# The first expert block's rows made by products of the resident x with marked lanes, and w2 of expert 0 waiting for its place alone

## The reference

```
h = modulate(rms_norm(x, norm_ffn_g[l]), sh_f, sc_f).reshape(-1, d)          # 512 x 1024
...
g_logits = (h @ w_group).astype(jnp.float32) + b_group.astype(jnp.float32)   # 4 groups
g_idx = jnp.argmax(g_logits, axis=-1)
e_logits = ((h @ w_router).astype(jnp.float32) + b_router...)                # 4 x 8 experts
within = jnp.take_along_axis(e_logits, g_idx[:, None, None], axis=1)[:, 0]
top_vals, top_idx = lax.top_k(within, MOE_TOP_K)                             # 2 of 8
...
for e in range(MOE_EXPERTS):                                                 # 32 experts
    hid = jax.nn.silu(h @ w1[e]) * (h @ w3[e])                               # 1024 -> 512
    out = out + gates[:, e:e + 1] * (hid @ w2[e]).astype(jnp.float32)        # 512 -> 1024
x = x + g_f * f.reshape(x.shape)
return rms_norm(x, final_norm_g)
```

## Time and profile before

| | before |
|---|---|
| median of 3 runs | 1003.13 us (1002.63 to 1018.23) |
| profiled execution | 1004.4 us |
| its span | 1002.5 us |
| mean granted TensorE clock | 0.949 of 2.4 GHz |
| TensorE busy | 871.5 us (87%) |
| VectorE / ScalarE / GpSimd busy | 423.2 / 245.4 / 138.1 us |
| moved by DMA | 263.58 MB |

### The profile page before, as it was taken

How to read it: one execution, slowest core, us unless ns; L and a number is a source line. 1 busy time by engine, 2 the same in 40 slices (tenths; PEclk the granted TensorE clock), 3 DMA queues, 4 the chain that set the end, 5 groups by cost and what they waited for, 6 DMA issues and landing times.

```text
span 1002.5 us, 12704 instructions
## 1 busy us (share of the span) xinstructions
PE 871.5 (87%) x4421; PEld 435.2 (43%) x4421; DVE 423.2 (42%) x1082; ACT 245.4 (24%) x560; POOL 138.1 (14%) x373
## 2 busy tenths in 40 slices
PE   4699999999989989999879999999999977666860
PEld 2355546644445555446633444444444433332320
DVE  3586888544388646035721323222221321211226
ACT  5411023103267664114010111111111211111102
POOL 1401002020000000001010222122121321221210
PEclk9799999999999999999789999999999988989995
DMA  9952204366700320034859999999999999999946
GB/s 341 348 169 49 84 0 120 101 199 245 269 2 1 105 106 1 20 148 168 336 212 390 377 418 418 419 421 420 420 421 421 418 418 418 418 418 419 419 189 251
DMA packets 52613, 263.58 MB, mean 263 GB/s; under 512 B 11171, under 2 KB 13531, under 8 KB 25696
## 3 DMA queue, kind: packets, MB, share of 16 engines
q1 hardware_dynamic: 40320, 246.04, 60.9%
q0 software_dynamic: 12080, 17.00, 6.1%
q10 hardware_dynamic: 176, 0.05, 0.0%
HBM read 265.66 MB, written 22.01 MB: 287 GB/s over the span
## 4 chain that ended last, share of the span: by engine, by line
PE 43%; issue 38%; POOL 6%; DVE 5%; DMA 4%; ACT 2%; POOLq 1%; SPq 0%; DVEq 0%; ACTq 0%
PE PS L729 14%; PE PS L992 6%; PE PS L918 4%; DMA BIG<-in_w_mod 3%; POOL held L578 2%; PE PS L925 2%; PE PS L639 2%; PE PS L694 2%; PE PS L955 2%; POOL BIG L587 2%; PE PS L1078 1%; PE PS L964 1%; DMA BIG<-xh_d,gidx 1%; DVE sml L1941 1%; PE PS L802 1%
## 5 line engine op out<-in xcount | busy, mean ns | idle before, releaser
L729 PE MATMUL PS<-BIG 128*128 128x512 f32 (+2 forms) x352 | 139.8, 553 | 0.0
L729 PEld LDWEIGHTS PS<-BIG 128*128 128x128 f32 x352 | 64.2, 190 | 68.6 <-issue 68.3
L1178 PE MATMUL PS<-BIG,GM 128*64 128x512 f32 x336 | 79.0, 613 | 7.2 <-DMA BIG<-in_moe_w 6.0
L1159 PE MATMUL PS<-S5Z,QKV 128*128 128x512 f32 x192 | 83.4, 592 | 0.0
L1156 PE MATMUL PS<-BIG,QKV 128*64 128x512 f32 x288 | 64.2, 596 | 7.2 <-DMA BIG<-in_moe_w 5.5
L578 POOL TENSOR_TENSOR held<-held 1x1 f32<-1x1 f32 x147 | 27.1, 185 | 310.3 <-PE PS L1132 169.7
L2300 DVE TENSOR_TENSOR QKV<-PS,QKV 64x512 f32<-64x512 f32 x50 | 34.4, 688 | 81.3 <-PE PS L1178 51.9
L1481 ACT ACTIVATE QKV<-PS,fcp 128x128 f32<-128x128 f32 x128 | 48.3, 458 | 63.1 <-PE PS L1132 63.1
L1149 PE MATMUL PS<-BIG,QKV 128*32 128x256 f32 x768 | 47.8, 400 | 12.8 <-DMA BIG<-in_moe_w 12.8
L2280 DVE TENSOR_SCALAR QKV<-PS,fcp 128x128 f32<-128x128 f32 x128 | 43.7, 405 | 33.2 <-PE PS L1132 33.2
L992 PE MATMUL PS<-BIG 128*128 128x512 f32 x128 | 56.1, 595 | 0.0
(11 more groups left out here) (480 smaller groups left out, 1158.2 us busy)
## 6 DMA issues: line engine op xcount, KB each, us to landing
BIG<-in_moe_w SPq DMA_DIRECT2D x84, 1024.0 KB, 21.2
BIG<-in_moe_w SPq DMA_DIRECT2D x21, 2048.0 KB, 22.9
S5Z<-in_moe_w SPq DMA_DIRECT2D x40, 1024.0 KB, 18.7
BIG<-in_w_mod SPq DMA_DIRECT2D x12, 2048.0 KB, 7.9
S5Z<-in_moe_w SPq DMA_DIRECT2D x10, 2048.0 KB, 22.8
BIG<-in_w_in SPq DMA_DIRECT2D x3, 2048.0 KB, 17.4
QKV<-in_x SPq DMA_DIRECT2D x8, 512.0 KB, 11.3
BIG<-in_w_out SPq DMA_DIRECT2D x2, 2048.0 KB, 11.8
```

What stands on the lines that cost most here:

```text
L729: ins = mm(dst[:, c0:width], hT[:, k, tok], wslot(n, width)[:, k, c0:width], start=(k == 0), stop=(k == KD - 1))
L1159: ins = mm(bank(2 + m), hgT[:, k, :], w13(side)[:, m, k, :], start=(k == 0), stop=(k == KD - 1))
L1178: ins = mm(PS[64 * n:64 * n + 64, 2560:3072], hidT[:, k % 2, 64 * (k // 2):64 * (k // 2) + 64], w2s(side)[:, k, 512 * n:512 * (n + 1)], st ...
```

## The change

In place of the gather from DRAM, the turning and the copies by both engines, the rows of block 0 are made so: VectorE writes, for each of the four token tiles, a matrix `own` (128 tokens x 64 lanes) that has the token's reciprocal `sml[:, 36 + t]` where the token's larger position equals block 0's first position plus the lane, and zero elsewhere. TensorE multiplies the resident `XN` with it, 8 slices of the model dimension (read with a step of 8 elements) times 4 token tiles, 32 products; the result is turned already. ScalarE copies it in two parts (signals `picked` and `hg_tr`) to `hgT0`, which lies in the upper half of `GM`, with the same scale and shift, and gives both `hgT_a` and `hgT_d`. Block 0's up-projection reads `hgT0` and stands ahead of the wait for `routed` on TensorE. GpSimd's first gather is that of block 1. On VectorE the weights of the two choices are computed ahead of the wait for `filled`. On SyncE w2 of expert 0 no longer waits for `hg_in`.

```
--- before.py
+++ after.py
@@ -213,6 +213,9 @@
         ysb = QKV[:, 6144:7168]
         hid = GM[:, 0:512]
         hidT = GM[:, 512:1024].rearrange("p (k s) -> p k s", k=4)
+        own = GM[:, 0:256].rearrange("p (t l) -> p t l", t=NLT)
+        lanes_at = GM[:, 256:320]
+        hgT0 = GM[:, 512:1024].rearrange("p (k s) -> p k s", k=KD)
         sg = wglu[:, :, :].rearrange("p k n -> p (k n)")
         rt = S5Z[:, 8192:11520]
         logit = rt[:, 0:144].rearrange("p (t e) -> p t e", t=NLT)
@@ -415,7 +418,6 @@
                 load13(0, 2, 0, piece)
             sp.wait_ge(sem("slots"), 2)
             sp.wait_ge(sem("routed"), 1)
-            sp.wait_ge(sem("hg_in"), 16)
             load2(0, 2)
             last = sp.value_load(btab[0:1, NBLK + 2:NBLK + 3], min_val=0, max_val=NTRI) + 3
 
@@ -560,7 +562,7 @@
             pool.wait_ge(sem("xh_out"), 16 * NLT)
             st.settle()
             pool.wait_ge(sem("slots"), 1)
-            pool.tensor_copy(gidx[:, :], slots[:, 0:1, 0]).then_inc(sem("gidx"), 1)
+            pool.tensor_copy(gidx[:, :], slots[:, 1:2, 0]).then_inc(sem("gidx"), 1)
             pool.wait_ge(sem("gidx"), 1)
             pool.indirect_dma_start(hg, None, xh_d, bass.IndirectOffsetOnAxis(gidx[:, 0:1], 0),
                                     bounds_check=LAT - 1, oob_is_err=False).then_inc(sem("hg_in"), 16)
@@ -583,7 +585,7 @@
             def gather(b):
 
                 pool.tensor_copy(gidx[:, :], entry(b, 0)).then_inc(sem("gidx"), 1)
-                hold(sem("gidx"), b + 1)
+                hold(sem("gidx"), b)
                 pool.indirect_dma_start(hg, None, xh_d, bass.IndirectOffsetOnAxis(gidx[:, 0:1], 0),
                                         bounds_check=LAT - 1, oob_is_err=False).then_inc(sem("hg_in"), 16)
 
@@ -597,8 +599,6 @@
                 pool.indirect_dma_start(pair_d, bass.IndirectOffsetOnAxis(sidx[:, 0:1], 0), ysb, None,
                                         bounds_check=TOPK * LAT, oob_is_err=False).then_inc(sem("y_sc"), 16)
 
-            hold(sem("hg_tr"), 1)
-            gather(1)
             hold(sem("hg_tr"), 2)
             gather(2)
 
@@ -1104,7 +1104,15 @@
             mm(bank(6, NE, 192), qb_b[0:NE, :], opp128[0:NE, :], start=True, stop=False)
             mm(bank(6, NE, 192), hb_b[0:NE, :], tri128[0:NE, :], start=False, stop=True)
             mm(bank(6, NE, 224), hb_b[0:NE, :], ident[0:NE, 0:NE], start=True, stop=True).then_inc(sem("place"), 1)
-            warm(8)
+            warm(5)
+            pe.wait_ge(sem("own"), 1)
+            for k in range(KD):
+                for t in range(NLT):
+                    ins = mm(bank(k // 4, 64, (k % 4) * P), XN[:, t, :].rearrange("p (q k) -> p k q", k=KD)[:, k, :], own[:, t, :],
+                             start=(t == 0), stop=(t == NLT - 1))
+                if k == KH - 1:
+                    ins.then_inc(sem("picked"), 1)
+            ins.then_inc(sem("hg_tr"), 1)
             for k in range(TOPK):
                 pe.wait_ge(sem("spread"), k + 1)
                 for t in range(NLT):
@@ -1115,19 +1123,11 @@
             mm(PS[0:1, 3584:3584 + NBLK], ones[0:NE, 0:1], cmph[0:NE, :], start=True, stop=False)
             mm(PS[0:1, 3584:3584 + NBLK], wexp[0:NE, :], cmpq[0:NE, :], start=False, stop=False)
             mm(PS[0:1, 3584:3584 + NBLK], wexp[0:NE, :], cmpf[0:NE, :], start=False, stop=True).then_inc(sem("bt"), 1)
-            warm(3)
-
-            pe.wait_ge(sem("routed"), 1)
-
-            mixed = pe.value_load(btab[0:1, NBLK:NBLK + 1], min_val=0, max_val=NTRI) + 1
-            small = pe.value_load(btab[0:1, NBLK + 1:NBLK + 2], min_val=0, max_val=NTRI) + 2
-            last = pe.value_load(btab[0:1, NBLK + 2:NBLK + 3], min_val=0, max_val=NTRI) + 3
 
             def turn_rows(b):
-                pe.wait_ge(sem("hg_in"), 16 * b + 16)
-                if not isinstance(b, int) or b >= 1:
-                    pe.wait_ge(sem("hgT_a"), b)
-                    pe.wait_ge(sem("hgT_d"), b)
+                pe.wait_ge(sem("hg_in"), 16 * b)
+                pe.wait_ge(sem("hgT_a"), b)
+                pe.wait_ge(sem("hgT_d"), b)
                 for k in range(KD):
                     ins = tr(bank(k // 4, P, (k % 4) * P), hg.rearrange("p (q k) -> p k q", k=KD)[:, k, :], ident)
                 ins.then_inc(sem("hg_tr"), 1)
@@ -1152,12 +1152,20 @@
                         for m in range(2):
                             if size == "half":
 
+                                few = hgT0[:, k, :] if isinstance(b, int) else hgT[:, k, 64:128]
                                 r = slice(64 * m, 64 * m + 64)
-                                ins = mm(PS[r, 1024:1536].rearrange("p (m h) -> p m h", m=2), hgT[:, k, 64:128],
+                                ins = mm(PS[r, 1024:1536].rearrange("p (m h) -> p m h", m=2), few,
                                          w13(side)[:, :, k, 256 * m:256 * m + 256], start=(k == 0), stop=(k == KD - 1))
                             else:
                                 ins = mm(bank(2 + m), hgT[:, k, :], w13(side)[:, m, k, :], start=(k == 0), stop=(k == KD - 1))
                     ins.then_inc(sem("w13_used"), 1)
+
+            up(0, "half", 0, 1)
+            pe.wait_ge(sem("routed"), 1)
+
+            mixed = pe.value_load(btab[0:1, NBLK:NBLK + 1], min_val=0, max_val=NTRI) + 1
+            small = pe.value_load(btab[0:1, NBLK + 1:NBLK + 2], min_val=0, max_val=NTRI) + 2
+            last = pe.value_load(btab[0:1, NBLK + 2:NBLK + 3], min_val=0, max_val=NTRI) + 3
 
             def turn_hid(b, size):
                 pe.wait_ge(sem("hid"), b + 1)
@@ -1192,10 +1200,6 @@
                 down(b - 1, size_before, j, i)
                 turn_hid(b, size)
 
-            warm(3)
-            turn_rows(0)
-            warm(2)
-            up(0, "half", 0, 1)
             turn_rows(1)
             turn_hid(0, "half")
             with pe.Fori(1, mixed + 1) as i:
@@ -1468,8 +1472,14 @@
                   bank(4, P).rearrange("p (h b c a) -> p b h a c", h=2, b=2, a=8)[:, b], ACT.Copy).then_inc(sem("e_exp"), 1)
 
 
+            act.wait_ge(sem("perm_in"), 16)
+            for piece, (signal, done) in enumerate((("picked", "hgT_a"), ("hg_tr", "hgT_d"))):
+                act.wait_ge(sem(signal), 1)
+                for k in range(KH * piece, KH * (piece + 1)):
+                    ins = A(hgT0[:, k, :], bank(piece, 64, (k % 4) * P), ACT.Identity, scale=fcp[:, 0, k:k + 1], bias=fcp[:, 1, k:k + 1])
+                ins.then_inc(sem(done), 1)
+
             act.wait_ge(sem("routed"), 1)
-            act.wait_ge(sem("perm_in"), 16)
 
             mixed = act.value_load(btab[0:1, NBLK:NBLK + 1], min_val=0, max_val=NTRI) + 1
             small = act.value_load(btab[0:1, NBLK + 1:NBLK + 2], min_val=0, max_val=NTRI) + 2
@@ -1510,7 +1520,6 @@
 
 
             act.wait_ge(sem("slots"), 2)
-            rows_T(0)
             step(0, "half")
             with act.Fori(1, mixed + 1) as i:
                 for j, size in enumerate(("half", "full", "quarter")):
@@ -2181,6 +2190,10 @@
             for i in range(2):
                 st(ts(virt[:, i:i + 1], n_all, -1.0 - i, None, ALU.add))
             st.settle()
+            dve.wait_ge(sem("e_exp"), 3)
+            st(ts(left, virt[:, 0:1], float(P), None, ALU.mult))
+            st.settle()
+            st(ts(lanes_at, lanes[:, 0:64], left, None, ALU.add))
             dve.wait_ge(sem("place"), 1)
 
             placed = bank(6, NLT * NE).rearrange("p (t e) -> p t e", t=NLT)
@@ -2201,13 +2214,19 @@
             st.settle()
             st(V.tensor_reduce(pos, picked, AX.X, ALU.add))
             st.settle()
+            st(tt(wts[:, 7, :], pos[:, 0], pos[:, 1], ALU.max))
+            st.settle()
+            for t in range(NLT):
+                ins = ts(own[:, t, :], lanes_at, wts[:, 7, t:t + 1], sml[:, 36 + t:37 + t], ALU.is_equal, ALU.mult)
+                if t < NLT - 1:
+                    st(ins)
+            ins.then_inc(sem("own"), 1)
             st(ts(blk, pos, -(P - 1) / 2.0, 1.0 / P, ALU.add, ALU.mult))
             st.settle()
             st(ts(blk, blk, MAGIC, MAGIC, ALU.add, ALU.subtract))
             st.settle()
             st(stt(pos, blk, -float(P), pos, ALU.mult, ALU.add))
             st.settle()
-            dve.wait_ge(sem("e_exp"), 3)
             for k in range(TOPK):
                 where, which = blk_of[k][:, :, 1, :], blk_of[k][:, :, 0, :]
                 st(tt(where, bc(virt, NLT, 1), bc(blk[:, k], NBLK, 2), ALU.is_equal))
@@ -2224,6 +2243,16 @@
             st.settle()
             ts(cmph[0:NE], virt[0:NE, :], endv[0:NE, 2:3], None, ALU.is_ge).then_inc(sem("cmp"), 1)
 
+            dve.wait_ge(sem("g_exp"), 1)
+            dve.wait_ge(sem("e_exp"), 1)
+            st(V.tensor_reduce(wts[:, 3, :], gra, AX.X, ALU.add))
+            st(ts(wts[:, 2, :], wts[:, 4, :], 1.0, None, ALU.add))
+            st.settle()
+            st(tt(wts[:, 3, :], wts[:, 3, :], wts[:, 2, :], ALU.mult))
+            st.settle()
```

(14 more changed lines are left out.)

85 lines of the change are left out of this document (51 added, 34 removed).

## The result

The change is slower: 1006.62 us, median of 8 runs (1005.53 to 1008.28), against 1002.38 us of the kernel before in the same rounds; the ratio is 1.0054, 95% interval 1.0039 to 1.0069. One run of the kernel before (1018.23 us) lay 2% above the fastest of it and is left out of the ratio as slow. The profiled execution took 1005.98 us, its span 1004.2 us (before 1002.5). In the rounds of the experiments the kernel before had medians of 1000.5 to 1002.5 us, so every experiment is read by its ratio to the runs of before that it shares.

What follows compares the result with a forecast made beforehand. The weight stream filling the DMA engines was taken to bound the kernel. A stream starting 3.2 us earlier plus 0.7 us from a later hole gave 3.9 us, from 1003.13 to 999.2 us, range 997.5 to 1003.2.

Steps and rivals of the forecast that it cites:

- the price of a pass of the marked-lane products: TensorE, the 32 new products for block 0's rows: 64 passes at 0.126 us each, taken as 8.0 us.
- The upper bound of 0.2125: TensorE, the marked-lane products priced by the turning at half clock: 0.2125 us a pass, 13.6 us.
- no hole: TensorE ahead of the marked-lane products: five warming products end at 496.1, just behind `own` at about 495.8.
- The lane products behind them: TensorE behind the marked-lane products: lane products take 1.9 us more, read by VectorE at 506.1.
- the forecast of 509.1: The time of `routed`: 5.2 us later than before, from `slots` 6.0 later less 0.76 saved on VectorE.
- The point from which the change loses: Marked-lane products on TensorE: over 11.2 us, 0.175 a pass, putting `routed` at 512.3.
- Rival A: TensorE's marked-lane products at half clock, up to 13.6 us, `routed` at 517.3, kernel at 1008.1 us; chance 0.08.
- VectorE: Seven new small instructions, 1.05 us, `own` at about 495.8; the way from `filled` to `routed` falls from 3.7 to 2.95.
- SyncE: w2 of expert 0 issued at 509.2, next transfer within 2 us; one stream hole, none at 512 to 518 or 552.
- The scalar loads: TensorE behind block 0's up-projection: three loads lie bare for 2.2 us, until 515.7.
- What the end follows: The weight stream's start: block 3's weights flow behind w2, from 516.0 instead of 519.2, a gain of 3.2 us.
- the holes downstream: In the weight stream, the small hole at 552 to 554 closes, 0.7 us more.

Runs made afterwards that it cites:

- the last version: The change with marked lanes stationary, contiguous x moving in two column groups, turning afterwards and silu's table loaded early: 997.3 us, ratio 0.9951 to the kernel before.
- the kernel with w2 alone: The kernel before with one edit, w2 of expert 0 not waiting for the gather of block 0: ratio 1.0019 to the kernel before.

## Why the prediction was wrong

**The step that failed is the price of a pass of the marked-lane products.** The prediction took 0.126 us, from the turning of gathered rows, "since the operand's step is the same". It measured 0.239: 15.3 us in place of 8.0, and filling the hole did not help (ratio 1.0060). The upper bound of 0.2125 came from the same transposes at half clock, and did not hold the value either. The step of the operand is the same, the form isn't: turned by products, the same rows cost 0.244 a pass. The contiguous row at 0.110 was right for a contiguous operand (0.111). The page of the Trainium skill that the prediction weighed was put aside as agreeing in sign; it names the penalty that decided, without a figure, and the row it was weighed against was one in which that penalty doesn't show.

**A second step failed beside it: "no hole".** The five warming products were timed by an execution in which the clock stood at 0.54 ahead of them. In the change it stood at 1.00, as in ten of the fourteen traces; the warming ended early, TensorE stood idle for 3.50 us, and the clock fell at about 497.5. Where the clock was low there, as in the run with half of the products (0.51 over 484 to 494), the same five took 5.47 us and left no hole. With the step's price the hole cost nothing on the products. With the price of a contiguous row it would have cost the gain: contiguous operands behind the same hole took 12.2 us in place of 7.0 and the ratio was 1.0027. The forecast needed both terms right, and had neither.

**The lane products behind them** took 3.64 us (510.89 to 514.53) in place of 1.9, at half clock. With 7.3 more for the products, 1.7 more for these and 0.5 less for the earlier start, `routed` came at 517.5, 8.4 later than the forecast of 509.1. The point from which the change loses, products over 0.175 a pass (11.2 us), is bracketed, not measured: with 7.7 us of products the kernel gained (0.9976), with 12.2 it lost (1.0027).

**Rival A** (chance 0.08) had the right sign, and nearly the time (1008.1), but not the cause. Half clock did come, but the strided products are as long without it; here it cost the 1.7 us of the lane products. For contiguous products its mechanism is real: 0.213 us a pass behind the fall, the 0.2125 of the prediction.

**VectorE**: right. `own` was there at 495.6 (495.8), and from reading the lane table to `routed` it took 517.52 - 514.63 = 2.89 us (2.95). **SyncE**: right, 1.96 us from w2's issue to the next (under 2), one hole in the stream, the small one at 552 closed.

**The scalar loads** on TensorE were priced at 2.2 us bare. They cost nothing: they run beside the products of the up-projection, and the turning of block 1 starts at 521.93, right behind it. **A wait that the prediction missed** is on ScalarE: its table for silu (1.28 us), loaded before during the first up-projection, now loads at 522.09 behind it, so that the up-projection of block 1 starts 3.92 us after the turning (521.93 to 525.85) and not 2.94, as before (520.64 to 523.58):

```profile
522.09 1.28 ACT L1502 ACT_TABLE_LOAD   x1 [9.67 <-PE PS L1157]
523.39 0.38 ACT L1502 ACTIVATE wglu<-PS 128x256 f32<-128x256 f32 x1
```

In the last version the one-element silu takes it away, and the distance is 2.94 again (511.01 to 513.95). Since other things were changed with it there, its own share of the end is not measured.

**What the end follows** was half right. The stream sets it, and nothing behind 600 us moves. But the prediction let block 3's bytes wait behind w2 (5.2 us) and gave the holes downstream 0.7 us. They are worth 4.1 us between 520 and 600. Another 1.7 us lie at the start: over the first 5 us behind the issue of block 3 the stream carries 272 GB/s in the kernel before and 411 in the change, where w2's bytes are still flowing. Together they take in w2's 5.2 us: the end goes with the issue of block 3's first transfer, that is, with the first half of block 0's up-projection or with `routed`, whichever is later, and hardly with the time at which w2 is out of the way. By that rule the forecast's own issue at 511.1 would have given a span of 511.1 + 485 = 996.1 in place of the forecast 998.6. Against that stands the 2.7 us by which the profiled execution of before was late: taken off, the gain in issue is 517.47 - 511.1 - 2.7 = 3.7 us. That it has to be taken off is argued, since no trace of the kernel before at full clock in the routing is there; the kernel with w2 alone, as fast, points the same way (its issue is 37.2 us behind the ten warming passes, that of before 40.6). So the two errors in the sum behind the products nearly cancel, and that contiguous operands with eleven warming products gained 5.0 where the prediction had 4.9 for that price is in part luck.

## What to carry to other kernels

A price has to be taken from a row of the same operation and form, not only of the same operand: here a transpose read the strided operand at half the cost of a product. Where a stationary float32 operand would have to be picked with a step of 4 elements or more, make it the moving one, read it contiguously, and leave the step to transposes behind it; this is what the last version does. And in a kernel whose end is set by a stream, look for the one issue that the end follows at a fixed distance; here what lay ahead of that issue was worth nearly its whole time, and w2 of expert 0, beside it, nothing. Check such a distance against ratios, not spans, since a delay ahead of both is in each span. And size warming products for the execution in which they end earliest, not for the one that was profiled.
